# Modulation products of a hybrid attention / gMLP / PEER block on one core: the two halves of a chunk go to TensorE unsummed, and ScalarE makes two terms

## The reference, cut to what matters

```python
mod = silu(c) @ w_ada + b_ada                 # 1024 -> 6144
sh1, sc1, gt1, sh2, sc2, gt2 = split(mod, 6)
h = rms_norm(x) * g_pre_mix * (1 + sc1) + sh1
z = h @ w_in                                  # q, k, v, su, sv
x = x + gt1 * rms_norm(concat(attention(q, k, v), gating(su, sv)) @ w_out)
h2 = rms_norm(x) * g_pre_ffn * (1 + sc2) + sh2
x = x + gt2 * rms_norm(peer(h2))              # 8 heads, top 16 of 16384 experts each
```

## Time and profile before

| | us |
|---|---|
| median of 3 runs | 1484.87 (1481.39 to 1485.45) |
| the profiled execution's own time | 1486.21 |
| its span, first to last instruction | 1484.4 |
| TensorE busy | 1434.3 (97%) |
| VectorE busy | 1169.5 (79%) |
| ScalarE busy | 655.9 (44%) |
| GpSimd busy | 576.7 (39%) |

### The profile page before, as it was taken

The page is one execution under the profiler, slowest core; times in us unless marked ns, Lnnn a source line. Parts: engine busy times, 40 slices in busy tenths (PEclk is TensorE's granted clock), DMA queues, the critical chain, the costliest instruction groups (busy, mean ns, idle before and its releaser), DMA issues.

```text
span 1484.4 us, 21726 instructions
## 1 busy us (share of the span) xinstructions
PE 1434.3 (97%) x7606; PEld 1273.3 (86%) x7606; DVE 1169.5 (79%) x2449; ACT 655.9 (44%) x1073; POOL 576.7 (39%) x462
## 2 busy tenths in 40 slices
PE   3999999999999999999999999999999999999998
PEld 3787468999999899999988888888888888888886
DVE  6987566577788889898667878887788788888887
ACT  3466233344444567677533333333333333333334
POOL 0000101244454458988723434443344343444440
PEclk9999999999999999999999999999999999999999
DMA  9965423446553468777899999999999999999993
GB/s 349 387 212 200 136 74 102 154 136 235 176 181 127 142 215 298 256 281 269 285 372 354 345 352 341 351 346 346 346 334 359 348 353 353 335 378 354 325 328 134
DMA packets 187709, 407.02 MB, mean 274 GB/s; under 512 B 13192, under 2 KB 100816, under 8 KB 185936
## 3 DMA queue, kind: packets, MB, share of 16 engines
q1 hardware_dynamic: 148016, 245.96, 47.7%
q0 software_dynamic: 36864, 134.23, 24.9%
q10 hardware_dynamic: 2720, 25.44, 4.6%
HBM read 362.59 MB, written 42.99 MB: 273 GB/s over the span
## 4 chain that ended last, share of the span: by engine, by line
PE 83%; POOL 5%; DVE 4%; issue 3%; ACT 2%; DMA 2%; SPq 0%; DVEq 0%; POOLq 0%; ACTq 0%
PE bank L1986 12%; PE bank L1987 12%; PE bank L1988 12%; PE bank L1913 10%; PE bank L1915 10%; PE bank L1914 10%; PE bank L1968 4%; PE bank L1855 3%; POOL gated L765 3%; PE bank L1882 2%; PE bank L1883 2%; PE bank L1881 2%; DVE part L1194 1%; PE bank L1903 1%; DMA ada<-in_w_ada 1%
## 5 line engine op out<-in xcount | busy, mean ns | idle before, releaser
L1913 PE MATMUL bank<-h2hi,dhi 128*128 128x384 f32 x1024 | 347.5, 339 | 6.1 <-DVE dlo L1378 5.9
L1915 PE MATMUL bank<-h2hi,dlo 128*128 128x384 f32 x1024 | 344.0, 336 | 0.0
L1914 PE MATMUL bank<-h2lo,dhi 128*128 128x384 f32 x1024 | 343.6, 336 | 0.0
L1986 PE MATMUL bank<-uhi,ahi 128*128 128x512 f32 x768 | 299.6, 390 | 2.9 <-DVE alo L1612 2.9
L1378 DVE TENSOR_TENSOR dlo<-down,dhi 128x1024 fp32r<-128x1024 f32 x128 | 165.5, 1294 | 171.3 <-ACT dhi L925 171.1
L1987 PE MATMUL bank<-ulo,ahi 128*128 128x512 f32 x768 | 299.4, 390 | 0.0
L1988 PE MATMUL bank<-uhi,alo 128*128 128x512 f32 x768 | 299.3, 390 | 0.0
L717 POOL DMA_INDIRECT rows<-in_peer_up,ids x128 | 162.8, 1272 | 239.0 <-DVE y L1455 207.0
L717 POOL DMA_INDIRECT rows<-in_peer_down,ids x128 | 159.9, 1250 | 217.9 <-DVE rows L1446 200.6
L925 ACT ACTIVATE dhi<-down 128x1024 fp32r<-128x1024 f32 x128 | 134.9, 1055 | 209.5 <-PE bank L1915 208.0
L1913 PEld LDWEIGHTS bank<-h2hi,dhi 128*128 128x128 f32 x1024 | 192.9, 188 | 10.4 <-DVE dlo L1378 7.5
(11 more groups left out here) (239 smaller groups left out, 2035.2 us busy)
## 6 DMA issues: line engine op xcount, KB each, us to landing
down<-in_down_t SPq DMA_DIRECT2D x128, 512.0 KB, 5.3
up<-in_peer_up SPq DMA_DIRECT2D x128, 512.0 KB, 7.4
ada<-in_w_ada SPq DMA_DIRECT2D x48, 512.0 KB, 9.9
gate<-gates_dram SPq DMA_DIRECT2D x32, 768.0 KB, 11.1
gates_dram<-stage ACTq DMA_DIRECT2D x11, 2048.0 KB, 7.8
gel_dram<-gel SPq DMA_DIRECT2D x80, 192.0 KB, 3.0
gelu<-gel_dram SPq DMA_DIRECT2D x80, 192.0 KB, 6.4
wq<-in_peer_query SPq DMA_DIRECT2D x16, 512.0 KB, 5.3
```

Source lines behind the costliest of these rows:

```text
L1913: pe.matmul(bank[7 * s][:, 0:TD], dhi[s][:, k, :], h2hi[:, k, 0:TD], start=k == 0, stop=False)
L1914: pe.matmul(bank[7 * s][:, 0:TD], dhi[s][:, k, :], h2lo[:, k, 0:TD], start=False, stop=False)
L1915: last = pe.matmul(bank[7 * s][:, 0:TD], dlo[s][:, k, :], h2hi[:, k, 0:TD], start=False, stop=k == KT - 1)
L1986: pe.matmul(got[:], ahi[j][:, tokens], uhi[j][:, half], start=first, stop=False)
```

## The change

For chunks 0 to 3, VectorE leaves out line 1197. Its last two instructions of a chunk raise a semaphore each, `dve_even` for the even half and `dve_ada` for the odd one. TensorE multiplies both halves, the even one as soon as `dve_even` is there, and writes the odd one's columns 48 columns further on in `bank[0]`. VectorE adds `b_ada` and both sets of columns, 16 columns at a time, in two instructions of which the second waits for the first. In chunk 2, ScalarE makes the products of k = 0 and k = 1 in front of `xn1`, and VectorE starts at k = 2. Chunks 4 to 11 stay as they are.

```diff
@@ scalar, between the root and xn1
+            act.wait_ge(zeros_ok, 3)
+            act.wait_ge(dve, 2)
+            act.wait_ge(pe_ada, 1)
+            act.wait_ge(ada_in[ada_slot(BY_SCALAR)][0], 16 * ada_use(BY_SCALAR))
+            for k in range(2):
+                act.activation(part[BY_SCALAR % 2][:, k, :], ada[ada_slot(BY_SCALAR)][:, k, :], ACT.Identity,
+                               bias=kT[:, 0:1], scale=c_col[:, k:k + 1]).then_inc(act_ada, 1)
             act.wait_ge(dve_rms1, 1)
-            act.wait_ge(zeros_ok, 3)
@@ vector, multiply_ada
+                    if k < 2 and n == BY_SCALAR:
+                        ve.wait_ge(act_ada, k + 1)
+                        continue
...
-                    ch.mark(ve.scalar_tensor_tensor(out=dst[:, k % 2, :], in0=a[:, k, :], scalar=c_col[:, k:k + 1],
-                                                    in1=dst[:, k % 2, :], op0=ALU.mult, op1=ALU.add))
+                    term = ve.scalar_tensor_tensor(out=dst[:, k % 2, :], in0=a[:, k, :], scalar=c_col[:, k:k + 1],
+                                                   in1=dst[:, k % 2, :], op0=ALU.mult, op1=ALU.add)
+                    if n < 4 and k >= KT - 2:
+                        term.then_inc(dve_ada if k % 2 else dve_even, 1)
+                    else:
+                        ch.mark(term)
+                if n < 4:
+                    return
                 ch.wait()
                 ve.tensor_tensor(dst[:, 0, :], dst[:, 0, :], dst[:, 1, :], ALU.add).then_inc(dve_ada, 1)
@@ vector, bias
-            add_bias(SC1)
-            add_bias(SH1)
-            ch.wait()
+            both = 2 * KT
+            ch.link(ve.tensor_tensor(modc[:, 0:both], bank[0][:, 0:both], columns[:, ROW_B:ROW_B + both], ALU.add))
+            ch.link(ve.tensor_tensor(modc[:, 0:both], bank[0][:, ODD_AT:ODD_AT + both], modc[:, 0:both], ALU.add))
@@ tensor, ada_chunk
+                if n < 4:
+                    for side, ready in enumerate((dve_even, dve_ada)):
+                        pe.wait_ge(ready, n + 1)
+                        for j in range(4):
+                            col = 4 * ADA_ORDER[n] + j
+                            at = col + ODD_AT * side
+                            last = pe.matmul(bank[0][:, at:at + 1], part[n % 2][:, side, j * P:(j + 1) * P],
+                                             ones[:, 0:1], start=True, stop=True)
+                    last.then_inc(pe_ada, 1)
+                    return
```

More of the change, by code:

```diff
@@ L68 @@
 HEAD_STEPS = 3 * 20 + 12
+BY_SCALAR = 2
+ODD_AT = 48
 TB = 8
@@ L481, in build_block @@
         dve = sem("dve")
-        dve_ada = sem("dve_ada")
+        dve_ada, dve_even, act_ada = sem("dve_ada"), sem("dve_even"), sem("act_ada")
         dve_ms, dve_rms1, dve_mod, dve_h1, dve_wT = (
```

## The result

Ten runs of each kernel, side by side: 1489.1 us median with the change (1485.02 to 1494.23), 1484.36 before (1481.39 to 1489.12). The ratio is 1.0028, 95% interval 1.0015 to 1.004. Two later sets of times of the same changed kernel gave 1.0009 (0.9997 to 1.0022) and 1.0019 (1.0005 to 1.0033); the mean of the three is 1.0019, 2.8 us. (The ratio is an estimate over all executions and not the quotient of the two medians; the medians of the three sets lie 4.7, 3.3 and 2.8 us apart.) The kernel became slower in each of the three, by less than the 0.3% bound by these ratios, and the interval of the second takes in no change. 1488.1 had been forecast.

A forecast was written before the change was run, and what follows sets the result against it. TensorE was taken to bound the stretch ahead of the bias. Terms 0.17 + 1.50 + 1.51 + 0.12 = 3.30 us, added to the 1484.87 median, gave 1488.1 us; range 1484.8 to 1490.8.

The forecast's parts named there:

- What bounds the start: From 28.86 to 38.20 us TensorE's instructions set the end; VectorE has slack, 0.44 us at chunk 3's sum.
- Rival B: TensorE's clock rises early, from 29 us, and `w_low` at 37.7 is last before the bias; total -0.9, chance 0.06.
- C: Added products slip beside other weight loads, so TensorE is not the limit and `w_low` is last; -0.4, chance 0.05.
- VectorE's relief in chunk 2: Two products, 0.85 us, leave VectorE's queue; chunk 3 finished some 2 us before TensorE asks, which buys nothing.
- Chunk 1's sum: Ahead of the reciprocal on VectorE; without it the reciprocal comes 0.61 us earlier and `xn1` could start at about 23.55.
- ScalarE's terms: Two terms ahead of `xn1`, waiting for the load of chunk 2's first part; `xn1` starts at 24.33 against 24.16, +0.17.
- The added products: TensorE, chunks 2 and 3: 16 instructions each instead of 8, 0.188 us apiece, nothing hidden; +1.50 and +1.51.
- The bias: VectorE's second addition now waits for the first's result; +0.12 us, bounds 0 to 0.3.
- Carried to the end: From 38 to 126 us no engine wait is for a DMA, so the whole 3.3 us shift is carried.
- Rival A: TensorE's clock rises later in the key product; with ten more products at the lower level +5.3 us, chance 0.15.
- D: VectorE's relief is what counts: 3.2 us less if all on the path, 1481.7 us, chance 0.03.
- E: The shift is partly given back between 43 and 220 us, about half: 1486.5 us, chance 0.08.

The follow-up runs named there:

- the second and third profiles: The changed kernel run twice more with no edit; ratios to the kernel before 1.0009 and 1.0019.
- kept busy: Useless wide products added in TensorE's idle time: to the kernel before 0.9998, to the changed kernel 1.0015, to halves in idle time only 1.0004.
- halves in idle time only: Against the kernel before: only chunks 0 and 1 unsummed, no ScalarE terms, one more small add behind the bias; ratios 0.9992 and 1.0.

## Why the prediction was right

**What bounds the start.** Right where the clock stays low, which is in two profiles of three: the second and third profiles have TensorE without a gap from 28.95 to the bias. The slack of chunk 3's sum was real too, and small: in the kernel before, kept busy, TensorE waits for that sum and starts chunk 3's products at 36.13, 0.35 before the 36.48 of the kernel before. Without the added products (halves in idle time only) the bias moved forward by 0.5 to 0.7 and not more, stopped by the low part of the key weights at 37.5 to 37.7, as the rivals B and C had worked out. VectorE's relief in chunk 2 bought nothing, as forecast, though its slack was larger than the forecast 2 us: in the second profile it has finished chunk 3 at 34.45 and TensorE comes to it at 38.28.

**Chunk 1's sum, 0.61.** Mis-sized a little: in the first profile the reciprocal starts at 23.20, 0.76 earlier than in the earlier trace rows, and without ScalarE's terms `xn1` starts 0.86 earlier. The sum could start only when the terms ahead of it had ended (23.31, sum at 23.35); the reciprocal needs nothing of them and starts 0.08 before the last one's end.

**ScalarE's terms, +0.17.** `xn1` at 24.36 to 24.42 against 24.16 to 24.20: right, and so was the mechanism (the landing of chunk 2's first part, then two activations, 1.52 us for both). What TensorE sees of it is less, +0.09, because the four instructions of `xn1` fill 4.54 us in a row here instead of 4.65. One profile had the landing half a microsecond later, which was the upper bound.

**The added products, +1.50 and +1.51.** Right in place, too small in size: 3.20 and 3.22 against 1.50 and 1.51 are +1.70 and +1.71. The prediction divided the row by eight and called the 0.188 the time between starts. It is not: each instruction more costs 0.21, by these two rows and by 32 in 6.62. The 0.4 us missing from the sum (3.30 forecast, 3.7 at the key product: 43.97 against 40.31) is this. Of the 107 ns that the Trainium skill (TensorE: Matmul & The Clock Gate, section LDWEIGHTS) gives for a weight load the prediction said that the trace did not agree. At the higher clock 16 products fill the 1.70 us from 31.00 to 32.70, 0.106 each; at the lower it is twice that. So the figure fits the higher level, and the prediction had compared it with a row of the lower.

**The bias, +0.12.** Right within 0.03: from the first addition to the scale it is 0.42 (41.73 to 42.15) against 0.27 (38.22 to 38.49), +0.15. With this the parts add up: 0.09 + 1.70 + 1.71 + 0.15 = 3.65, and the key product is 3.66 later.

**Carried to the end.** Right up to 224 us: +3.57 at 77 us, +3.92 at 224. Behind that the scatter hides it in a single profile, and only the times of many executions speak. The 0.35 more arises near 115 us, in all three profiles of the changed kernel and not with either part alone. It is an idle time of VectorE of 0.46 us between two multiply-adds of the same chunk (line 1205), for which the profile names no other engine; its cause is open.

**Rival B, 0.06.** It came true in one profile of three, so its chance was too low, and its price was wrong: not -0.9 but +0.2 at 77 us. Its first half was right to a tenth (bias at 37.74 for 37.8). The second took for granted that a risen clock stays up through the idle time in front of the key product. The prediction had argued that unbroken work with few columns had not raised the clock before and so would not. That is still how most profiles go (with the products twice, unbroken work from 28.92 to 48.5 us did not raise it), but it is no rule: the same transposes did raise it in one execution of the changed kernel, and with the halves in idle time only it rose at 35.9 to 36.5 us in all three profiles (chunk 3's eight products in 1.13 to 1.33 us instead of 1.71), each time after 16 products for chunk 1 where there were 8. Without ScalarE's terms, with the same 16, it did not. Whether the added work or its timing decides is open. The Trainium skill's rule (TensorE: Matmul & The Clock Gate, section The HAM clock gate), activity releases and idleness throttles, agrees with these traces in direction: up to 260 us every rise fell in work and every fall in or just behind an idle time. By itself it does not say which work or which idle time will do it: 19.6 us of unbroken work passed without a rise, and the clock stayed up through 2.21 us of idle time in one kernel.

**Rival A** (a later rise): by the records of the granted clock the rise came at 48.3 and 47.3 in the second and third profiles, 4.3 and 3.2 us behind the start of the key product, against 4.5 in the kernel before: no later.

**Rivals C, D and E.** The added products don't slip beside the others (3.20 for 1.50). VectorE's relief is not what counts, as the bias came 3.5 later in spite of it. The shift was not given back between 43 and 220 us.

**The sum.** Three profiles average +2.8 at 224 us, 2.7 over the two of the kernel before; the three ratios average 1.0019, 2.8 us. That the time agrees with the forecast of 3.3 owes something to luck: the products cost more, and one profiled execution in three pays hardly any of it. By the medians, which lie 4.7, 3.3 and 2.8 us apart, it is 3.6.

## What to carry to other kernels

Work taken from an engine with slack and given to the one that sets the end is a loss even where it is little: here 3.2 us of VectorE's time (the prediction's own sum, in rival D) were bought with 3.4 us of TensorE's in front of the bias and 1.5 of ScalarE's. The same split is free in the chunks that TensorE multiplies while it waits, so look at each place of a loop by itself. And where the second half of a kernel scatters by more than the effect, compare the start of one instruction just behind the change in several profiles, before believing the difference of two spans. Look at the granted clock on the way, too: one fall of 3.4 us costs 1.6, half of this whole effect.

## What the runs showed of the hardware that was not expected

TensorE's clock can rise during transposes of 128 columns and products of one column, and it did so in one profiled execution and not in two others of the same program: from then on 12 transposes took 1.51 us instead of 2.80, and 16 products 1.84 instead of 3.41 (timeline durations). With the products issued twice, 19.6 us of such work without a break (28.92 to 48.5) did not raise it. It was down again behind idle times of 2.84 us in the first profile and 3.33, 2.42 and 1.83 in those kept busy, and still up behind 2.21 in the last of these. Between 241 and 255 us an idle time of 2.15 to 2.16 us is in every profile, and the clock fell behind it in 6 of 14. So the length of the idle time alone doesn't tell whether the clock falls. The idle time of 2.1 us in front of the key product of the kernel before, at the lower level, cannot show a fall. A weight load with one column behind it costs 0.21 us at the lower and 0.106 at the higher level, so such products follow the clock although they move next to no data.
